# Down projection of the feed-forward block by seven block products per pair of chunks

## The reference, cut to what matters

```
h2 = rmsnorm_2(x, g_ffn[l])
x = x + jnp.square(jax.nn.relu(h2 @ w_up[l])) @ w_down[l]
```

## Time and profile before

| | us |
|---|---|
| median of 3 runs (2828.24 to 2829.1) | 2828.27 |
| the profiled execution | 2825.38 |
| its span, first to last instruction | 2823.5 |
| TensorE busy, weight load busy | 2742.2, 2183.2 |
| VectorE, ScalarE, GpSimd busy | 1381.1, 1120.2, 913.7 |
| first matmul of the down projection | 2465.08 |

### The profile page before, as it was taken

How to read it: one execution, slowest core, us unless ns; L and a number is a source line. 1 busy time by engine, 2 the same in 40 slices (tenths; PEclk the granted TensorE clock), 3 DMA queues, 4 the chain that set the end, 5 groups by cost and what they waited for, 6 DMA issues and landing times.

```text
span 2823.5 us, 36713 instructions
## 1 busy us (share of the span) xinstructions
PE 2742.2 (97%) x13400; PEld 2183.2 (77%) x13400; DVE 1381.1 (49%) x1745; ACT 1120.2 (40%) x1563; POOL 913.7 (32%) x497
## 2 busy tenths in 40 slices
PE   6999999999999998999999999999999999999999
PEld 4788888787777776878877777777888888878887
DVE  7754443305777776591025555454446444443331
ACT  4211123324555544442246766765335333321110
POOL 1222222222555553222321211111125888622221
PEclk9999999999999999999999999999999999999999
DMA  5333321344112113113320100102432333343222
GB/s 227 133 128 120 118 89 52 112 139 145 60 53 82 52 53 119 52 60 112 119 93 31 38 30 30 38 30 83 178 142 90 111 111 119 134 164 105 89 89 89
DMA packets 73961, 269.53 MB, mean 95 GB/s; under 512 B 8208, under 2 KB 8848, under 8 KB 73360
## 3 DMA queue, kind: packets, MB, share of 16 engines
q1 hardware_dynamic: 73872, 268.39, 26.8%
HBM read 207.54 MB, written 60.82 MB: 95 GB/s over the span
## 4 chain that ended last, share of the span: by engine, by line
PE 66%; issue 23%; POOL 4%; ACT 3%; DVE 3%; DMA 1%; SPq 0%; POOLq 0%; ACTq 0%; DVEq 0%
PE PS L823 38%; PE PS L1307 10%; PE PS L1053 5%; POOL WL L2630 3%; PE PS L1025 2%; PE PS L958 2%; PE PS L987 2%; PE PS L1002 2%; PE PS L1211 2%; PE PS L1192 1%; PE PS L1151 1%; DVE bC L2263 1%; PE PS L1166 1%; DMA X<-xt 0%; ACT dAT L1788 0%
## 5 line engine op out<-in xcount | busy, mean ns | idle before, releaser
L2630 POOL TENSOR_TENSOR WL<-WR,WH 128x1024 fp32r<-128x1024 f32 x177 | 440.6, 2489 | 1609.7 <-ACT WH L1418 1502.4
L823 PE MATMUL PS<-HH,WH 128*128 128x512 f32 x1960 | 621.7, 398 | 20.2 <-POOL WL L2630 4.5
L823 PE MATMUL PS<-HL,WH 128*128 128x512 f32 x1960 | 606.6, 391 | 0.0
L823 PE MATMUL PS<-HH,WL 128*128 128x512 f32 x1960 | 605.3, 390 | 0.0
L823 PEld LDWEIGHTS PS<-HH,WH 128*128 128x128 f32 x1960 | 361.2, 189 | 107.4 <-issue 25.8
L823 PEld LDWEIGHTS PS<-HL,WH 128*128 128x128 f32 x1960 | 369.2, 188 | 78.8
L823 PEld LDWEIGHTS PS<-HH,WL 128*128 128x128 f32 x1960 | 368.7, 188 | 78.5
L1418 ACT ACTIVATE WH<-WR 128x1024 fp32r<-128x1024 f32 x177 | 187.6, 1060 | 578.7 <-PE PS L823 478.1
L2263 DVE TENSOR_TENSOR_SCAN bC<-bN,EPSC 128x256 f32<-128x256 f32 (+7 forms) x128 | 226.1, 1778 | 56.0 <-ACT bN L1604 52.8
L2654 POOL TENSOR_TENSOR bB<-bB,bC 128x256 f32<-128x256 f32 (+7 forms) x128 | 187.6, 1474 | 193.4 <-DVE bC L2263 193.4
L823 PE MATMUL PS<-GH,WH 128*128 128x512 f32 x536 | 166.1, 391 | 3.3 <-DVE GL L2024 3.3
(11 more groups left out here) (339 smaller groups left out, 4314.4 us busy)
## 6 DMA issues: line engine op xcount, KB each, us to landing
WR<-wst SPq DMA_DIRECT2D x179, 512.0 KB, 3.4
uRAW<-wst SPq DMA_DIRECT2D x33, 512.0 KB, 4.9
hid<-uQ SPq DMA_DIRECT2D x32, 512.0 KB, 2.6
TMP<-mods SPq DMA_DIRECT2D x24, 512.0 KB, 4.2
MR<-mods SPq DMA_DIRECT2D x24, 512.0 KB, 5.2
MRAW<-mods SPq DMA_DIRECT2D x16, 512.0 KB, 15.7
HLF<-hid SPq DMA_DIRECT2D x16, 512.0 KB, 4.5
GLF<-hid SPq DMA_DIRECT2D x16, 512.0 KB, 4.5
```

Source lines behind the costliest of these rows:

```text
L823: last = pe.matmul(PS[:, dst0 + q:dst0 + q + HALF], l, rr[:, k * S + q:k * S + q + HALF], start=a, stop=z)
L2630: pool.tensor_tensor(WL[slot][:, :], WR0[:, :], WH[slot][:, :].bitcast(F32), ALU.subtract).then_inc(w_lo, 1)
```

## The change

The down projection takes the form of the up projection. The hidden size is cut in eight passes of four chunks (two pairs), the output in four tiles of two chunks (`DOWNS` = 32 tiles, `PASS` = 4 tiles a pass). A tile is seven products, each two pairs x 3 = 6 matmuls of 512 columns, into the seven banks. The sums of each product are kept over the passes in SBUF (`DM[m][i]`, 28 of 128 x 512); in the last pass they are combined into the result. The residual is put into four of the seven sums at the start, and one subtraction makes it come out right.

The seven units per pair of hidden chunks are made when the pair is made: the three plain halves are stored by `store_halves`, the four differences by VectorE in `turn_hidden` and stored by `store_turned`. A pass loads its seven units (each two pairs side by side), and ScalarE and VectorE split them (`unit_hi`, `unit_lo`) a pass ahead, 2, 2, 2 and 1 per tile. Of the weight sums VectorE makes two (`down_sum`), GpSimd two (`combine`); GpSimd makes all low parts.

TensorE:

```diff
-            for q in range(FFQ):
-                down_pair(q, 0, first=True)
-                with pe.Fori(1, KT // 2 - (q == FFQ - 1)) as i:
-                    down_pair(q, i)
...
+            def down_product(i, e):
+                for kp in range(2):
+                    w = slice(kp * P, (kp + 1) * P)
+                    for n, (l, low) in enumerate(((DH, False), (DH, True), (DL, False))):
+                        last = pe.matmul(up_bank(i), l[i][:, w], right(i, kp + 2 * e, low),
+                                         start=kp == 0 and n == 0, stop=kp == 1 and n == 2)
                 return last
+            def down_pass(first_t, units, e, first=False):
+                for m in range(PASS):
+                    t = first_t + m
+                    for i in range(7):
+                        pe.wait_ge(up_hi, 7 * t + (7 * UPS + i + 1))
+                        pe.wait_ge(up_lo, 7 * t + (7 * UPS + i + 1))
                         if m == 0:
+                            pe.wait_ge(r_lo, units + (i + 1))
+                        if not (first and m == 0):
+                            pe.wait_ge(dn_e, 7 * t + (i - 6))
...
+                        down_product(i, e).then_inc(up_p, 1)
```

SP, from the last pairs of the up projection to the end:

```diff
+                if n:
+                    store_turned(n - 1)
+                store_halves(n)
             sp.wait_ge(up_lo, 7 * (UPS - 1))
...
+            load_down(0)
+            load_down(1)
             end = 7 * (UPS - 1)
             sp.wait_ge(up_p, end + 1)
...
+            load_right(0, 0)
+            store_turned(UPS - 2)
+            for i in range(1, 4):
+                sp.wait_ge(up_p, end + i + 1)
+                load_right(0, i)
+            load_sums(0)
+            for i in range(4, 7):
+                sp.wait_ge(up_p, end + i + 1)
+                load_right(0, i)
+            store_halves(UPS - 1)
+            load_sums(1)
             for m in range(2):
                 sp.wait_ge(st_h[m], 16 * UPS)
...
+            store_turned(UPS - 1)
+            load_sums(2)
+            sp.wait_ge(st_t, 32 * UPS)
+            load_sums(3)
+            for t in range(DOWNS):
+                e, m = t // PASS, t % PASS
+                if t < DOWNS - 2:
+                    sp.wait_ge(up_lo, 7 * (UPS + t + 1))
+                    load_down(t + 2)
+                if m == 0 and e < DOWNS // PASS - 1:
+                    sp.wait_ge(up_p, 7 * (UPS + t))
+                    for i in range(7):
+                        load_right(e + 1, i)
```

ScalarE:

```diff
+            def down_pass(t, half, loads, e, last=False):
+
+                for m in range(PASS):
+                    if not last:
+                        for i in ((0, 1), (2, 3), (4, 5), (6,))[m]:
+                            unit_hi(loads, 1 - e, i)
+                    if last and m == PASS - 1:
+                        return
+                    for i in range(7):
+                        down_weights_hi(t + (m + 1), (m + 1) % 2, half + (m + 1) // 2, i)
```

VectorE:

```diff
+            def turn_hidden(n, first=False):
+
+                lower, upper = slice(0, HALF), slice(HALF, S)
+                dve.wait_ge(up_q, 2 * n + 2)
+                if not first:
+                    dve.wait_ge(st_t, 32 * n)
+                dve.tensor_tensor(UT[0][:, lower], UQ[0][:, upper], UQ[0][:, lower], ALU.subtract).then_inc(up_t, 1)
...
+            def down_pass(t, half, done, e, first=False):
+
+                for m in range(PASS):
+                    if first:
+                        dve.wait_ge(xf_move[m], 96)
...
+                        links(dve.tensor_tensor(DM[m][6][:, :], DM[m][6][:, :], DM[m][5][:, :], ALU.subtract))
...
+                    for i in range(3):
+                        down_add(t + m, m, i, first)
+                    down_sum(t + (m + 1), (m + 1) % 2, half + (m + 1) // 2, 2)
+                    for i in range(3, 6):
+                        down_add(t + m, m, i, first)
+                    down_sum(t + (m + 1), (m + 1) % 2, half + (m + 1) // 2, 5)
+                    if first and m == 0:
+                        turn_hidden(UPS - 1)
+                    for i in ((0, 1), (2, 3), (4, 5), (6,))[m]:
+                        unit_lo(done, 1 - e, i)
+                    down_add(t + m, m, 6, first)
```

GpSimd, per tile:

```diff
+                lo(0, a11)
+                lo(1, a12)
+                combine(3, by_blocks(DLF[2]), a11)
+                lo(2)
+                combine(4, a12, by_blocks(DLF[3]))
+                lo(3)
+                lo(4)
+                lo(5)
+                lo(6, a22)
```

More of the change, by code:

```diff
@@ L386, in alternate, with down_block, unit @@
             return t[:, :].rearrange("p (k two q) -> p k two q", two=2, q=P)[:, :, j, :]
+        def down_block(par, n, j):
+            return D_RAW[par][:, n * HALF:(n + 1) * HALF].rearrange("p (k two q) -> p k two q", two=2, q=P)[:, :, j, :]
         def by_blocks(t):
             return t[:, :].rearrange("p (k q) -> p k q", q=P)
[L391 to L398, removed]
+        def unit(e, i, plain=False, low=False):
+            t = (HLF, GLF)[e] if plain else ((HH, GH), (HL, GL))[low][e]
+            return kt(t, i)
         ld_c = sem("ld_c")
@@ L771, in _ @@
[L771 to L781, removed]
@@ L1367, in half_step @@
-            def half_step(slot, pair, q, h, k):
-                high, low, _, at = D_TILES[q % 2][k]
-                b, c0 = slice(k * P, (k + 1) * P), h * HALF
-                for n, (l, rr) in enumerate(((WH, high), (WH, low), (WL, high))):
-                    last = pe.matmul(PS[:, pair * S + c0:pair * S + c0 + HALF], l[slot][:, b],
-                                     rr[:, at * S + c0:at * S + c0 + HALF], start=k == 0 and n == 0, stop=k == KT - 1 and n == 2)
-                return last
@@ L2556, in relu_scaled, with up_pair @@
                                          op0=ALU.max, op1=ALU.mult).then_inc(up_e, 1)
-            def up_pair(n, first=False, between=()):
+            def up_pair(n, first=False, second=False, last=False):
                 def fill(at):
-                    for k in (between[at] if between else ()):
-                        hidden_lo(0, k)
+                    if at == 0 and not first:
+                        turn_hidden(n - 1, first=second)
+                    if not last:
+                        return
+                    if at == 0:
+                        down_sum(0, 0, 0, 2, first=True)
+                    if at == 1:
+                        down_sum(0, 0, 0, 5, first=True)
+                    for i in ((), (0, 1), (), (2, 3), (4, 5, 6))[at]:
+                        unit_lo(28, 0, i)
                 e = 9 * n
@@ L2600, in _ @@
             up_pair(0, first=True)
-            with dve.Fori(0, (UPS - 2) // 2) as i:
+            up_pair(1, second=True)
+            with dve.Fori(1, (UPS - 2) // 2) as i:
                 for m in range(2):
-                    up_pair(2 * i + (1 + m))
-            up_pair(UPS - 1, between=((0,), (1, 2), (3, 4), (5,), (6, 7)))
-            dve.wait_ge(ld_xf, 16 * KT)
-            for n in range(DOWN - 1):
-                s = (C_FF + n) % 2
-                dve.wait_ge(chunk_done, C_FF + n + 2)
-                x = kt(X, n % KT)
-                dve.tensor_tensor(x, PAIR[s], x, ALU.add).then_inc(free[s], 1)
-                if n < DOWN - KT:
-                    hidden_lo(n // KT + 1, n % KT)
```

316 lines of the change are left out of this document (184 added, 132 removed).

## The result

The changed kernel takes 2858.57 us (median of 4 runs, 2853.25 to 2860.81) against 2828.26 us in the same comparison: ratio 1.0106, 95% interval 1.0089 to 1.0124. It is slower by 1.06%, 30.3 us. The forecast was 2834 us with a range up to 2857; the direction was right, the size was not.

What follows compares the result with a forecast made beforehand. TensorE was taken as the bound, busy for 97% of the span at full clock. Terms -41.3 + 16.2 + 20.4 + 10.6 = +5.9 us on 2825.4 gave 2831.3, forecast as a median of 2834 us, range 2811 to 2857.

Steps and rivals of the forecast that it cites:

- Term 1: Down projection: 1344 matmuls instead of 1536, -41.3 us.
- Term 4: Last pass: VectorE needs 12.6 us a tile against TensorE's 9.6, +10.6 us, bounds +4 and +20.
- No long idle stretch: Sign of a misread queue: no TensorE idle stretch of 17 to 25 us behind the first 42 down matmuls.
- waits in most tiles: Sign against the forecast: TensorE waits in most down tiles, meaning GpSimd and VectorE bind.
- Helpers in time: Faster rival: six boundary waits of 1 us or less, last pass +6, 2815 us; chance 0.24 with cases in between.
- GpSimd and VectorE become the bound: Slower rival in the down tiles: VectorE needs 10.4 us a tile on average, 2849 us; chance 0.2.
- The turn is short: Rival: without ScalarE's two units ahead of tile 1's weights, the turn costs about 0, 2818 us; chance 0.03.
- Term 3: Boundaries of passes 1 to 6: TensorE waits 3.4 us at each second tile, +20.4 us in all.
- 5.1 us to the first unit: Pass boundary: step from the low part of product 6 being ready to the next pass's first unit landing, 5.1 us.
- by that rule the later waits of 3 us could each pay too: Later TensorE waits: idling drops it to half clock, so each might cost extra; the trace showed 1.00 behind 2.79 us.
- Term 2: Turn from up to down projection: 20.5 us idle plus 2.5 of lowered clock, less 6.8 before, +16.2 us.
- tile 0 is well prepared and ends at 2465.1 + 9.6: Turn: the first down tile runs without delay in 9.6 us, ending at 2474.7.

Runs made afterwards that it cites:

- e6: e3 with the last pass's seven combinations per tile left out and the uncombined sums stored: 2788.35 us.
- e1: Changed kernel with the next pass's seven unit loads issued ahead of SP's wait and the weight loads in passes 1 to 6: 2817.33 us.
- e3: Changed kernel with both reorderings of SP's queue, those of e1 and e2, together: 2798.43 us.
- e4: Changed kernel with ScalarE and VectorE splitting the next pass's units 0, 2, 2, 3 per tile instead of 2, 2, 2, 1: 2812.07 us.
- e9: Changed kernel with the seven unit loads ahead of the two weight loads, still behind SP's wait for the sixth low part: 2831.09 us.
- e5: Changed kernel with 18 filler matmuls into an unused PSUM bank before the second tile of passes 1 to 6: 2846.25 us.
- e7: e3 with pass 0's units 0 and 1 loaded ahead of a turned store, tile 1's weights and the first residual later: 2794.49 us.
- e10: Changed kernel with only units 0 and 1 issued behind the two weight loads, units 2 to 6 once unit 0 is copied: 2857.70 us.
- e2: Changed kernel with SP issuing pass 1's unit loads and tile 2's weights earlier at the turn from up to down projection: 2839.32 us.
- e11: e7 with VectorE's sum of product 6 in pass 0's first tile ahead of two low parts of pass 1's units: 2794.75 us.

## Why the prediction was wrong in size

**What held.** Term 1 (192 matmuls for 0.2275 us each), the up projection at no cost, and steady tiles bound by TensorE with VectorE and GpSimd just inside held. The three places of loss (one long stretch, six boundaries, the last pass) were right, and so was the work that each waits for; sizes and two steps within them were not. Term 4, +10.6, measures 8.2 in the ledger and 10.1 in e6: a tile of 11.8 us, not 12.6, since the waits for GpSimd, nine at 0.25 us in the forecast, came to less. "No long idle stretch" and "waits in most tiles", which would have shown a misreading, did not occur. The rivals "Helpers in time", "GpSimd and VectorE become the bound" and "The turn is short" are out; e1 and e3 exclude the second, for they have TensorE busy for 99.9% of the steady stretch. The first needed boundary waits under 1.4 us, which came only when SP's order or the spread of the units was changed (e1, e3, e4 and what builds on e3).

**Term 3 was mis-sized, 20.4 for 40.0 us, in two steps.** The first is "5.1 us to the first unit": it was 7.1. I read 5.0 us off a unit load that stood behind one weight load, and at the boundary two of them are ahead. The bytes ahead are the same, 512 KB in one load there and in two here, but the changed kernel moves smaller packets: 1.9 KB on average from 2584 to 2600 us (4.12 MB in 2151 packets), where the row I read comes from a stretch with 3.6 KB (5.77 MB in 1581, 2450 to 2470 us). Which of the two, the number of loads or the size of their packets, costs the 2 us was not tested. Issue at +2.5 instead of +3.4 us gave back 0.9, and the other parts of the chain were within 0.2 us; so each wait came to 4.5 instead of 3.4. e9 shows what the loads in front cost. The second is the clock, which was at hand and which the sum put at nothing for the boundaries: "by that rule the later waits of 3 us could each pay too". I went by 1.00 behind the single 2.79 us wait. At 4.1 to 5.2 us each wait did pay, 1.7 to 2.8 us, and e5 gives 12.3 us for the six. Whether six waits of 3.4 us would have paid is open: near that length the runs show both (see the last section).

**Term 2 was 16.2 for 24.3 us.** Tile 1 starts 39.4 us after the first down matmul, and the forecast had 30.1 (2495.2 less 2465.1). The chain of waits runs through VectorE and SP, and two of its steps make up the difference. VectorE has the low parts of pass 0 done at 2482.97, 14.5 us after the first down matmul, where I had 7.9 (2473.0 less 2465.1). And the first unit of pass 1 came in 6.9 us after its issue at 2496.63, behind two weight loads, where I had 4.3, the same landing step as in term 3. The first of these is also why "tile 0 is well prepared and ends at 2465.1 + 9.6" failed: tile 0 took 6.9 us longer. SP issues tile 1's weights ahead of unit 0, the stores of a turned tile ahead of unit 1 and the residual ahead of unit 4, so ScalarE got unit 1 only at 2467.06, and the low part of unit 2 ended a wait of 3.88 us. e7 takes 3.6 us off tile 0 by moving loads alone. The idle stretch itself, 22.9 for 20.5 us, looks nearer than the working was, because its start was late by most of what its end was.

**The range** ended at 2857 because the slow rival was a bound on VectorE and GpSimd; the upper bounds of terms 2 and 3 (+4.5 and +12.6) would have led from 2834 to 2851 by themselves. No case had the half clock at every boundary, which is the one that came.

## What to carry to other kernels

When a change moves loads across a boundary between passes, follow the in-order queues in both directions: what stands *ahead* of the first needed load on its DMA queue, and what an engine has ahead of work whose operands are already there. Here a reorder of SP's issues, with the same arithmetic, turned +1.1% into -1.0% (e3), and into -1.2% with the first units' loads moved too (e7). Where TensorE is the bound, price a wait of 4 us or more with the half clock behind it, in this kernel about half as much again; a filler of useless matmuls shows that part alone. Where another engine sets the pace, as VectorE does in tile 0, the half clock cost nothing.

## What the runs showed of the hardware

- Waits of 1.66 us (e9) and 1.68 us (e7) left TensorE at 0.23 us per matmul; those of 3.88 us and over in the changed kernel were followed by matmuls at 0.43 us, some 2 us more for them in all. Between 2.9 and 3.8 us both occur, and the length does not decide it: waits of 3.10 (e10), 3.69 (e9) and 3.75 us (e2) kept the full pace, those of 2.90 (e11), 3.08 (e7), 3.51 (e4) and 3.76 us (e6) did not. The one of 3.08 us in e7 had it for four matmuls and then fell to 0.43, though the matmuls had already resumed.
- The first of seven 512 KB loads was in after 3.7 us (e1) or 4.0 us (e9) with no load just ahead of it, and 6.3 us with two 256 KB weight loads directly in front; without five of the loads behind it, it was 6.1 us (e10). In the trace of before, a unit load issued 0.37 us behind one load of the same 512 KB was in 4.6 us after its issue.
- VectorE and GpSimd were busy for 89% and 88% of 228 us (e1), with short operations that take two SBUF inputs on both, and TensorE waited for neither.
